# Router stage of a two-layer trunk on one core: who normalises the tokens, and in what order

## The reference, cut to what matters

```python
x = x + g1 * out
h = _rms(x, norm_g[l, 1]) * (1.0 + sc2) + sh2
x = x + g2 * moe(h, router_w, router_b, moe_w_gate[l], moe_w_up[l], moe_w_down[l])
...
def moe(h, router_w, router_b, w_gate, w_up, w_down):
    t = h.reshape(bn * L, d)
    scores = jax.nn.softmax((t @ router_w).astype(f32), axis=-1)
    biased = (scores + router_b.astype(f32)).reshape(-1, N_GROUPS, EXPERTS_PER_GROUP)
    group_score = lax.top_k(biased, TOP_K)[0].sum(-1)
    grp = jnp.argmax(group_score, axis=-1)
    ...
    wsel = wsel / jnp.sum(wsel, axis=-1, keepdims=True)
    gates = jnp.sum(jax.nn.one_hot(idx, N_EXPERTS, dtype=f32) * wsel[..., None], axis=1)
    ...
```

## Time and profile before

| | |
|---|---|
| three executions | 838.25, 841.78, 842.1 us (median 841.78) |
| profiled execution | 839.53 us; span in the profile 837.6 us |
| busy: PE, PEld, DVE, ACT, POOL | 810.8 (97%), 507.3 (61%), 279.3 (33%), 175.3 (21%), 37.9 us (5%) |
| chain that ended last | PE 82%, DMA 10%, DVE 6%, ACT 1% |
| weights | 290.10 MB read, 348 GB/s over the span |
| router stages in the span | about 203 to 220 us and 590 to 605 us |

### The profile page before, as it was taken

One profiled execution on the slowest core, in us unless ns is written; L12 is line 12 of the kernel. 1 busy time (PEld: TensorE's weight loads), 2 busy tenths in 40 slices (PEclk: granted clock), 3 DMA queues, 4 the chain that ended last, 5 costly groups with the idle time before them and its releaser, 6 DMA issues.

```text
span 837.6 us, 13390 instructions
## 1 busy us (share of the span) xinstructions
PE 810.8 (97%) x5780; PEld 507.3 (61%) x5780; DVE 279.3 (33%) x586; ACT 175.3 (21%) x307; POOL 37.9 (5%) x67
## 2 busy tenths in 40 slices
PE   4999999999999999999999999999899999999997
PEld 3877778986555355525546888798653554355534
DVE  2255524415632121212125844581641212121213
ACT  4066014411501110111014112300411101110111
POOL 4100100030300000000000000000120000000000
PEclk8999999999999999999999999999999999999999
DMA  9999875986799999999999979366589999999992
GB/s 342 370 338 367 301 257 201 375 285 223 300 404 425 423 420 425 428 418 425 425 413 385 348 253 336 115 234 268 207 341 419 423 425 421 425 422 424 428 418 112
DMA packets 69221, 292.54 MB, mean 349 GB/s; under 512 B 4017, under 2 KB 6182, under 8 KB 48628
## 3 DMA queue, kind: packets, MB, share of 16 engines
q1 hardware_dynamic: 67156, 289.70, 87.7%
q10 hardware_dynamic: 1248, 1.08, 0.5%
q0 software_dynamic: 768, 1.04, 0.4%
HBM read 290.10 MB, written 1.70 MB: 348 GB/s over the span
## 4 chain that ended last, share of the span: by engine, by line
PE 82%; DMA 10%; DVE 6%; ACT 1%; issue 1%; SPq 0%; DVEq 0%
PE ps L1978 23%; PE ps L2008 11%; DMA ring<-in_moe_w_up 9%; PE ps L2123 7%; PE ps L1951 6%; PE ps L1541 5%; PE ps L1604 4%; PE ps L2023 4%; PE ps L1738 3%; PE ps L1598 3%; PE ps L1826 3%; PE ps L1579 3%; PE ps L2119 1%; DVE xT L1206 1%; PE ps L1725 1%
## 5 line engine op out<-in xcount | busy, mean ns | idle before, releaser
L1978 PE MATMUL ps<-ring,arena 128*64 128x512 f32 x832 | 224.1, 593 | 3.8 <-DMA ring<-in_moe_w_up 3.6
L1978 PEld LDWEIGHTS ps<-ring,arena 128*64 128x64 f32 x832 | 71.9, 137 | 112.6 <-issue 110.1
L2008 PE MATMUL ps<-ring,arena 128*64 128x512 f32 x512 | 113.4, 595 | 0.5 <-ACT arena L855 0.5
L2008 PEld LDWEIGHTS ps<-ring,arena 128*64 128x64 f32 x512 | 35.3, 137 | 66.6 <-issue 64.0
L1328 DVE SCALAR_TENSOR_TENSOR arena<-ps,arena 128x256 f32<-128x256 f32 x32 | 20.0, 669 | 154.8 <-PE ps L1978 154.8
L2123 PE MATMUL ps<-hs,ring 128*128 128x256 f32 x320 | 70.3, 380 | 0.0
L2123 PEld LDWEIGHTS ps<-hs,ring 128*128 128x128 f32 x320 | 60.5, 190 | 9.3 <-issue 1.4
L1951 PE MATMUL ps<-arena 128*128 (+1 forms) x512 | 60.5, 276 | 0.0
L1951 PEld LDWEIGHTS ps<-arena 128*128 128x128 f32 x512 | 58.6, 192 | 2.1 <-issue 1.6
L1978 PE MATMUL ps<-hs,arena 128*64 128x512 f32 x128 | 56.3, 593 | 0.0
L1338 DVE TENSOR_TENSOR arena<-ps,arena 128x512 f32<-128x512 f32 x28 | 18.0, 686 | 97.6 <-ACT arena L861 97.6
(11 more groups left out here) (312 smaller groups left out, 869.5 us busy)
## 6 DMA issues: line engine op xcount, KB each, us to landing
ring<-in_moe_w_up SPq DMA_DIRECT2D x64, 1024.0 KB, 18.5
ring<-in_moe_w_down SPq DMA_DIRECT2D x64, 1024.0 KB, 15.1
ring<-in_mod_w SPq DMA_DIRECT2D x24, 2048.0 KB, 13.5
ring<-in_moe_w_gate SPq DMA_DIRECT2D x20, 2048.0 KB, 15.9
hs<-in_moe_w_gate SPq DMA_DIRECT2D x8, 2048.0 KB, 17.6
ring<-in_hy_in_w SPq DMA_DIRECT2D x6, 2048.0 KB, 14.7
ring<-in_ab_in_w SPq DMA_DIRECT2D x4, 2048.0 KB, 12.8
arena<-in_moe_w_gate SPq DMA_DIRECT2D x4, 2048.0 KB, 16.8
```

The lines of the kernel that those rows point to most:

```text
L1978: ins = mm(bank(4 + w)[e * 64:e * 64 + 64, :], xg[:, k, e * 64:e * 64 + 64], weights[:, k, :], start=(k == 0), stop=(k == KD - 1))
L2008: ins = mm(bank(6 + half)[e * 64:e * 64 + 64, :], hidT[:, f, e * 64:e * 64 + 64], down_unit(n + 4 + e)[:, f, half * 512:half * 512 + 512], ...
```

## The change

It touches the router stage of both layers, on four engines.

- ScalarE: the second half of the squares is done in two instructions of 512 columns, the first of them after three of the four residual parts. After the exponential it copies the rows of 1/rms from bank 3 to `rstd` in SBUF. `hT` is made for k = 4, then 5, 6, 7, then 3. `htm` is copied in halves of k (4 to 7 first) for both streams, in four instructions of 512 columns.
- VectorE: the division of the scores comes ahead of the products; these read `rstd` and cover k = 3, 4 and then k = 5, 6, 7. The reciprocal and product for `gate` and the first mod row stand behind the first part of `S`.
- GpSimd: it makes the products for k = 0, 1, 2 itself, from `rstd`, as soon as the copy is there.
- TensorE: it also waits for the copy, and signals the turned blocks by halves of k.

```diff
@@ gpsimd
-                pool.wait_ge(q["d_xn"], xn_done(2 * l + 1, 1))
+                pool.wait_ge(q["a_re"], 2 * l + 2)
+                link(pool, "g_chain", g.tensor_tensor(sq[:, 0:3], xT[:, 0:3], rstd[:].rearrange("p (o s) t -> p o s t", o=1).broadcast_to([P, 3, NS, T]), ALU.mult))
@@ scalar, squares
+                if n % 2 and half:
+                    act.wait_ge(q["d_x"], x_done(n - 1, half) - 1)
+                    act_fn(sqf[:, 1024:1536], xf[:, 1024:1536], ACT.Square)
+                    sl = slice(1536, 2048)
+                    act.wait_ge(q["d_x"], x_done(n - 1, half))
                 act_fn(sqf[:, sl], xf[:, sl], ACT.Square).then_inc(q["a_sq"], 1)
@@ scalar, moe
                 act_fn(R["e"], R["lg"], ACT.Exp).then_inc(q["a_re"], 1)
+                act.wait_ge(q["t_sw"], 3 * l + 3)
+                nc.scalar.copy(rstd[:].rearrange("p s t -> p (s t)"), bank(3)[:, 0:256]).then_inc(q["a_re"], 1)
...
-                scaled(n, (4, 5))
-                scaled(n, (6, 7))
+                scaled(n, (4,))
+                scaled(n, (5, 6, 7))
                 scaled(n, (3,))
...
-                for s in range(NS):
-                    act.wait_ge(q["t_htm"], 2 * l + s + 1)
-                    nc.scalar.copy(M["htm"][:, s * 1024:s * 1024 + 1024].rearrange("p (k r) -> p k r", k=KD),
-                                   bank(2 * s, 2).rearrange("p (r k) -> p k r", k=KD)).then_inc(q["a_htm"], 1)
+                for i, half in enumerate((1, 0)):
+                    act.wait_ge(q["t_htm"], 2 * l + i + 1)
+                    for s in range(NS):
+                        ins = nc.scalar.copy(htm[:, s].rearrange("p (k h r) -> p h k r", k=KD, h=2)[:, half],
+                                             bank(2 * s + half).rearrange("p (r k) -> p k r", k=KD))
+                    ins.then_inc(q["a_htm"], 1)
@@ vector, moe
-                dve.wait_ge(q["t_sw"], 3 * l + 3)
-                rows = bank(3)[:, 0:256].rearrange("p (o s t) -> p o s t", o=1, s=NS)
-                for ks in (slice(4, 8), slice(0, 4)):
-                    v.tensor_tensor(sq[:, ks], xT[:, ks], rows.broadcast_to([P, 4, NS, T]), ALU.mult).then_inc(q["d_xn"], 1)
-                dve.wait_ge(q["a_re"], l + 1)
+                dve.wait_ge(q["a_re"], 2 * l + 1)
                 L(v.tensor_reduce(R["c2"], g3(R["e"]), AX.X, ALU.add))
                 L(v.reciprocal(R["c2"], R["c2"]))
                 L(v.tensor_tensor(g3(R["score"]), g3(R["e"]), col(R["c2"], NE), ALU.mult))
+                dve.wait_ge(q["a_re"], 2 * l + 2)
+                rows = rstd[:].rearrange("p (o s) t -> p o s t", o=1)
+                for a, b in ((3, 5), (5, 8)):
+                    v.tensor_tensor(sq[:, a:b], xT[:, a:b], rows.broadcast_to([P, b - a, NS, T]), ALU.mult).then_inc(q["d_xn"], 1)
...
-                L(v.reciprocal(R["c3"], R["c3"]))
-                L(v.tensor_tensor(g3(R["gate"]), g3(R["w"]), col(R["c3"], NE), ALU.mult))
-                take_mod(LAST_MODS[l][0])
...
                     if a == 0:
+                        L(v.reciprocal(R["c3"], R["c3"]))
+                        L(v.tensor_tensor(g3(R["gate"]), g3(R["w"]), col(R["c3"], NE), ALU.mult))
...
+                        take_mod(LAST_MODS[l][0])
                         take_mod(LAST_MODS[l][1])
@@ tensor, moe
                 pe.wait_ge(q["d_xn"], xn_done(2 * l + 1, 1))
+                pe.wait_ge(q["a_re"], 2 * l + 2)
...
-                        if k == 3:
-                            ins.then_inc(q["t_htm"], 1)
+                    if k % 4 == 3:
+                        ins.then_inc(q["t_htm"], 1)
```

More of the change, by code:

```diff
@@ L666, in squares @@
                 sl = slice(half * 1024, half * 1024 + 1024)
-                if n:
+                if n and not (n % 2 and half):
                     act.wait_ge(q["d_x"], x_done(n - 1, half))
+                elif n:
+                    pass
                 elif half:
@@ L689, in scaled @@
                 l, i = n // 2, n % 2
-                act.wait_ge(q["d_xn"], xn_done(n, int(min(ks) >= 4) if n == 0 else int(min(ks) < 4)))
+                act.wait_ge(q["d_xn"], xn_done(n, int(min(ks) >= 4 if n == 0 else max(ks) > 4)))
                 for k in ks:
```

## The result

The changed kernel takes 843.79 us (median of 22 executions, 841.83 to 846.22), the kernel before 840.25 us in the same comparison (22 executions, 838.25 to 843.23). The ratio is 1.004, with a 95% interval of 1.003 to 1.005: slower by some 3.5 us. That is inside the 0.5% that the prediction called no change, and three times the 1.10 us that it had worked out. The median also lies just inside the stated range (up to 844.0), but that end had been set by the spread of single executions and a longer product, not by what happened.

What follows compares the result with a forecast made beforehand. TensorE, busy 97% of the span, was taken to bound the kernel, so only its standstills could be won. First stage +1.12, second +0.42 and squares -0.44 gave +1.10 on 840.42: 841.5 us, range 837.4 to 844.0.

Steps and rivals of the forecast that it cites:

- What bounds, and that the stages' loss passes on whole: Whole kernel: TensorE bounds it, busy 97% of the span; what a router stage wins or loses reaches the end whole.
- Squares in quarters, -0.44: Second router stage: ScalarE's squares done in smaller parts end earlier, -0.44 us; worth nothing in the first stage.
- Fewer columns and the division ahead: Both router stages: VectorE's 1280 columns take 1.55 us, not 2.35; with division ahead, bias -1.01 us (second), -0.54 (first).
- behind the mask, worth 0: Both router stages: moving the reciprocal, product and first mod row behind the first slots gains 0 to -0.1 us, taken as 0.
- The sum without interference: Both router stages, GpSimd not hindering VectorE: squares -0.44, second stage -1.01, first stage -0.27, together -1.72 us.
- the sum with exclusion: Both router stages, VectorE and GpSimd excluding each other: +1.12 first, +0.42 second, squares -0.44, together +1.10 us; chance 0.55.
- rival 1: Both router stages: GpSimd does not exclude VectorE, so -1.72 us, 838.7 us in all; chance 0.3.
- GpSimd beside VectorE: Both router stages: GpSimd's 768-column product takes 1.43 us and excludes VectorE's two-SBUF-input instructions, costing 0 to 1.43 us per layer.
- rival 2: Second router stage: TensorE's clock falls during the longer mask wait, slowing mod row and pack, +5.9 us, 846.3; chance 0.05.
- 3 (an earlier mask wins nothing because `hT` and `htm` decide): Both router stages: ScalarE's copies set the slots, so only the squares count, about -0.4 us, 840.0; chance 0.1.

Runs made afterwards that it cites:

- rest_only: The changed kernel without the shared normalising: products as before, GpSimd only scales; squares, copies and moved weights' division stay. 841.18 us, ratio 0.9998 to before.
- filler: The changed kernel with five idle TensorE products of 256 columns in the second stage, before the turned blocks; 843.12 us, ratio 1.0018 to before.
- all_vector: The changed kernel, but VectorE also makes the products for k = 0, 1, 2 from SBUF and GpSimd makes none; 840.56 us, ratio 0.9994 to before.
- psum_products: The changed kernel, but TensorE makes the 1/rms rows twice and VectorE's products read them from PSUM, ahead of the division; 840.97 us, ratio 1.0006 to before.
- double_product: The changed kernel with GpSimd's product of 768 columns done twice, one after the other; 846.71 us in one execution.
- by_stage_fill: by_stage with three idle TensorE products of 256 columns added in the second stage's waits; 841.58 us, ratio 1.0009 to before.
- by_stage: The changed kernel without GpSimd's product: first stage's products from PSUM before the division, second stage's all on VectorE from SBUF; 840.36 us, ratio 0.999 to before.

## Why the prediction was right or wrong

**What bounds, and that the stages' loss passes on whole: right.** 369.9 us lie between the packs of stage 1 and the last residual of stage 2 in both traces. The stages' losses, 1.48 and 2.17, make 3.65, and the medians lie 3.54 apart.

**Squares in quarters, -0.44: right.** -0.42 in the changed kernel's chain (TensorE's squares start 1.84 us after the last residual part instead of 2.27).

**Fewer columns and the division ahead: right as durations** (1.56 us for 1280 columns; division 0.19 when alone), and **behind the mask, worth 0: right** (stage 1 of rest_only is unchanged).

**The sum without interference has a slip.** In the first stage it lets the pack follow the mod row, -0.27. By the same steps that the sum with exclusion uses, `htm` would be there at 217.76 + 2.05 = 219.81, so the pack could win only 0.14: rival 1's -1.72 should have been -1.59. The forecast does not rest on it.

**GpSimd beside VectorE: the mechanism was right, its size too small.** The step took 1.43 us for the product of 768 columns, by proportion from the gate product; it takes 1.82. The row it was scaled from the earlier trace rows has an input that is one value repeated along 64 columns, while both inputs of this product change from column to column: 2.4 ns a column against 1.9. Whether that or a fixed part of each instruction makes the difference, no run separates. The estimate by the Trainium skill's figure, 1.69 (GPSIMD Engine Reference, Elementwise — side-by-side cycle accounting; the figure is that of an addition), was nearer. In stage 1 the longer product is the miss: +1.12 forecast, +1.48 measured, 0.36 apart, and the product is 0.39 longer. The range for one layer had been left at 1.43 as its upper end, and 1.82 lies over it.

**Stage 2: the step that failed.** The prediction gave -0.02 there (+0.42 for the exclusion, -0.44 for the squares), held that the mask would set the mod row and the pack, and put the clock at nothing, since "the wait grows by only 0.4 us". Measured: +2.17.

For the mask the number came out exact: it ends 13.50 us after the last residual part, 13.51 before. That is luck. GpSimd's product was 0.39 longer than taken, and the copy of the rows began 0.40 earlier than the squares alone give (6.11 us after the last residual part, not 6.51), because the broadcast product met the upper clock (0.70 us in place of 1.22). In filler, where it took 1.22, the mask ends at 13.71.

But the mask no longer decided. TensorE turns the blocks before it counts positions and starts the last mod row, and the prediction compared `htm` with the mod row's end, never the blocks with its start:

- Late `hT`. ScalarE began 9.17 us after the last residual part, where it began 8.20 before. The prediction's 605.4 for `htm` has this delay in it (603.9 and GpSimd's 1.43 us), but it drew no wait of TensorE from it. The last ten blocks could start only at 604.56. At the upper clock (1.39 us) they would have been done near 605.95, and the mod row some 0.2 us late: an estimate, from the rows of both kernels.
- The clock. This is the larger part. The wait that grew by 0.4 was that for the mask; the one for the first block grew from nothing to 2.3 us, and the granted clock was at its lower level under the blocks and most of the last mod row. The ten blocks took 2.39 us in place of 1.39, the mod row 3.00 in place of 1.95: about 2.05 of the 2.17 us. This was rival 2, at 0.05, argued away on the wrong wait. filler took 1.18 off. The pack, which the rival had priced at 3.8 more, was back at the upper level and cost nothing.

Late `hT` and the clock need each other: in rest_only the ten blocks also took 2.39 us, but they started ahead of the mask and were done 0.3 us after it, so that the fall cost some 0.5 us there. Mod row start +1.17, mod row +1.05: that is stage 2's 2.17, less 0.05. That the exclusion leads to the loss is shown (all_vector and psum_products, without it on the way to `hT`, have 15.19 and 15.30). Why the clock fell where it did stays open.

GpSimd's six scalings, which the prediction kept at 2.78 us, took 4.12. That was not on the path: the last ended at 604.63, before TensorE had come to their blocks.

**Rivals.** 1 (no exclusion) fell: the division waits. 3 (an earlier mask wins nothing because `hT` and `htm` decide) was half right, in that `hT` decides in stage 2. 2 was right about the clock and the mod row, and its 846.3 overpriced the pack.

## What to carry to other kernels

Before work is moved to GpSimd, list what VectorE does in that stretch. Here every VectorE instruction with two inputs in SBUF that came second to GpSimd's long product stood until it ended, however short it was itself, and so did a tensor by a scalar from SBUF to SBUF. The price was what was left of GpSimd's product on VectorE's chain, and moving the product's start only moved it to the next such instruction. A product moved out of PSUM into SBUF so that GpSimd can share it joins that list: from PSUM VectorE's products ran beside GpSimd's (psum_products), from SBUF one was held by it (double_product). And when one engine's chain gets longer, look at every wait of TensorE that hangs on it, not only at the one on the path now: find where TensorE stands still longest, and price what follows at the lower clock too.

## What the runs showed of the hardware that was not expected

- A GpSimd product of 768 float32 columns with two changing inputs takes 1.81 to 1.83 us in each of the seven kernels that have it (but 2.36 for double_product's second, which VectorE held up); one of 1024 with an input repeated along 64 columns takes 1.90.
- VectorE and GpSimd wait for whole instructions of each other, but not always in turns: a VectorE product slipped between two GpSimd products (double_product), while GpSimd's first scaling waited out two VectorE products in a row, 1.79 us in place of 0.46 (changed kernel). GpSimd's scalings of 128 columns lengthened VectorE's first ranking instruction by 0.14 us at most.
- A VectorE tensor-by-scalar of 16 columns waited 1.73 us beside GpSimd's product, while a reduction and a reciprocal (0.18 and 0.17 us) and products with one input in PSUM ran unhindered, and GpSimd memsets hindered nothing.
- The granted clock fell in different places of the same code in different executions (stage 1 of the changed kernel's order: mod row 1.95 and 2.49 us), and in by_stage_fill, with idle matmuls in one wait, it fell under the blocks instead (15.58 against by_stage's 15.07). In the six traces of stage 2 in which TensorE stood still before the blocks, for 0.57 to 3.81 us, the last mod row was slowed (2.20 to 3.04 us), and in none of the other seven.
